# Three of eight residual tiles multiplied by the norm's factor on GpSimd

## The reference, cut to what matters

```python
def _rmsnorm(x, g):
    xf = x.astype(jnp.float32)
    y = xf * lax.rsqrt(jnp.mean(xf * xf, axis=-1, keepdims=True) + EPS)
    return (y * g.astype(jnp.float32)).astype(x.dtype)
...
            h = _rmsnorm(x, norm_pre_mix[i]) * (1.0 + sc1) + sh1
            mix, na, nb, ns = _token_mixer(h, ...)
            x = x + g1 * _rmsnorm(mix, norm_post_mix[i])
            h = _rmsnorm(x, norm_pre_ffn[i]) * (1.0 + sc2) + sh2
            ...
            x = x + g2 * _rmsnorm(f, norm_post_ffn[i])
```

## Time and profile before

| | |
|---|---|
| median of 3 executions | 2082.62 us (2078.98 to 2089.65) |
| profiled execution | 2081.15 us |
| its span in the profile | 2079.2 us |
| TensorE, VectorE, ScalarE, GpSimd busy | 93%, 59%, 41%, 10% of the span |
| first residual, Exp's end to the next norm's Ln | 505.83 to 519.83 us |
| second residual, the same | 941.63 to 955.63 us |
| third residual, the same | 1423.69 to 1437.69 us |

### The profile page before, as it was taken

One profiled execution on the slowest core, in us unless ns is written; L12 is line 12 of the kernel. 1 busy time (PEld: TensorE's weight loads), 2 busy tenths in 40 slices (PEclk: granted clock), 3 DMA queues, 4 the chain that ended last, 5 costly groups with the idle time before them and its releaser, 6 DMA issues.

```text
span 2079.2 us, 36179 instructions
## 1 busy us (share of the span) xinstructions
PE 1923.7 (93%) x13204; PEld 1709.5 (82%) x13204; DVE 1236.0 (59%) x1783; ACT 846.4 (41%) x1030; POOL 217.6 (10%) x317
## 2 busy tenths in 40 slices
PE   4999999989999999996999999896499999999994
PEld 3888989987899999995889989895387877888883
DVE  3677667645523223336776676555566566888886
ACT  4332222443422122225332222535355456777774
POOL 3101221200000000001102112100100000000020
PEclk9999999999999999998999999998699999999998
DMA  9642333353333233325724333323448566999994
GB/s 335 232 163 93 131 131 121 117 192 136 111 131 137 106 122 131 121 81 190 253 94 139 125 110 119 134 97 121 174 123 282 186 219 234 361 379 383 381 384 171
DMA packets 146667, 376.94 MB, mean 181 GB/s; under 512 B 9712, under 2 KB 47024, under 8 KB 146080
## 3 DMA queue, kind: packets, MB, share of 16 engines
q1 hardware_dynamic: 119824, 274.61, 38.4%
q0 software_dynamic: 26768, 101.28, 13.5%
HBM read 340.06 MB, written 35.80 MB: 181 GB/s over the span
## 4 chain that ended last, share of the span: by engine, by line
PE 81%; DVE 6%; DMA 5%; issue 4%; ACT 3%; POOL 1%; DVEq 0%; POOLq 0%; ACTq 0%; SPq 0%
PE ps L1913 35%; PE ps L1921 17%; PE ps L2216 15%; PE ps L2237 4%; DMA rawr<-w_gu 2%; PE ps L1934 2%; PE ps L2079 1%; DMA adaw<-w_ada 1%; PE ps L2067 1%; PE ps L2082 1%; PE ps L2080 1%; PE ps L1944 1%; DVE wlr L1746 1%; DVE wreg L1273 1%; PE ps L1953 1%
## 5 line engine op out<-in xcount | busy, mean ns | idle before, releaser
L1913 PE MATMUL ps<-h_hi,whi 128*128 128x272 f32 x2368 | 501.0, 293 | 17.3 <-DVE h_lo L1235 17.3
L1913 PE MATMUL ps<-h_lo,whi 128*128 128x272 f32 x2368 | 494.1, 290 | 0.0
L1913 PEld LDWEIGHTS ps<-h_hi,whi 128*128 128x128 f32 x2368 | 374.6, 190 | 62.4 <-issue 41.6
L1746 DVE TENSOR_TENSOR wlr<-rawr,whr 128x2048 fp32r<-128x2048 f32 (+1 forms) x162 | 321.9, 1992 | 121.6 <-ACT whr L1040 117.7
L1183 DVE TENSOR_TENSOR wlo<-raw,whi 128x1024 fp32r<-128x1024 f32 (+1 forms) x180 | 229.5, 1275 | 266.2 <-ACT whi L780 263.8
L1913 PEld LDWEIGHTS ps<-h_lo,whi 128*128 128x128 f32 x2368 | 375.0, 190 | 0.0
L780 ACT CAST whi<-raw 128x1024 fp32r<-128x1024 f32 (+1 forms) x180 | 193.6, 1076 | 356.6 <-PE ps L1921 356.6
L1040 ACT CAST whr<-rawr 128x2048 fp32r<-128x2048 f32 (+1 forms) x162 | 269.2, 1668 | 155.7 <-PE ps L2237 86.5
L1921 PE MATMUL ps<-h_hi,wlo 128*128 128x272 f32 x2368 | 320.5, 288 | 0.0
L1921 PEld LDWEIGHTS ps<-h_hi,wlo 128*128 128x128 f32 x2368 | 306.4, 188 | 0.0
L2216 PE MATMUL ps<-whr,hu_hi 128*128 128x512 f32 (+1 forms) x432 | 167.3, 387 | 7.2 <-DVE yu L1810 4.5
(11 more groups left out here) (405 smaller groups left out, 2604.7 us busy)
## 6 DMA issues: line engine op xcount, KB each, us to landing
rawr<-w_gu SPq DMA_DIRECT2D x90, 1024.0 KB, 9.4
adaw<-w_ada POOLq DMA_DIRECT2D x48, 1024.0 KB, 8.7
rawr<-w_dn SPq DMA_DIRECT2D x54, 768.0 KB, 9.9
raw<-w_mix SPq DMA_DIRECT2D x64, 512.0 KB, 3.6
raw<-w_gu SPq DMA_DIRECT2D x44, 512.0 KB, 3.4
raw<-w_out SPq DMA_DIRECT2D x32, 512.0 KB, 3.5
y_rows<-tables POOLq DMA_DIRECT2D x26, 512.0 KB, 2.9
raw<-w_xbc SPq DMA_DIRECT2D x24, 512.0 KB, 4.3
```

The costliest lines, as they stand in the source:

```text
L1746: v.tensor_tensor(ring_group(wlr, g).rearrange("p k s c -> p s k c"), raw_group(g), ring_group(whr, g).bitcast(F32).rearrange("p k s c -> ...
L1913: mm(ps[:, 2 * s + half, 0:HALF], whi[:, s, k * P:(k + 1) * P], a[:, k, half * HALF:(half + 1) * HALF], start=(n < 2), stop=False)
```

## The change

In the three residuals the products of tiles 5, 6 and 7 leave VectorE. GpSimd has a new function `late_tiles`, which waits for the same `rstd_ready` and makes these three products into the same places of `sq`, each with an increment of a new semaphore `late_scaled`. VectorE makes the first five products as before and waits for `late_scaled` ahead of the additions of tiles 5, 6 and 7. GpSimd's calls stand at the head of layer 1, ahead of the wait for x's spill (for the second residual), and in each layer after the wait for the windows (`windows_out`): in layer 0 that is behind the eight loads of modulation weights and ahead of the memset of the zeros.

```diff
         ADDED = {}
+        LATE, LATE_SET = (KT - 3, KT - 2, KT - 1), {(0, POST_MIX): 0, (0, POST_FFN): 1, (1, POST_MIX): 2}
...
         @block.gpsimd
         def _(pool):
+            def late_tiles(L, idx, src):
+
+                pool.wait_ge(rstd_ready, NORMS * L + idx + 1)
+                for k in LATE:
+                    nc.gpsimd.tensor_tensor(sq[:, k, 0:SEQ], src[:, k, 0:SEQ], rstd[:, 0:SEQ], ALU.mult
+                                            ).then_inc(late_scaled, 1)
+
...
             for L in range(DEPTH):
                 if L:
 
+                    late_tiles(0, POST_FFN, f)
                     pool.wait_ge(x_ready, 2 * KT * L)
                     pool.dma_start(x_spill, xreg[:, :]).then_inc(spill_out, 16)
...
                     pool.wait_ge(slabs_used, FIRST[0]["outB"] * 2 + PRIME)
                     ada_load(GAP, range(KT))
                 pool.wait_ge(windows_out, 64 * (L + 1))
+                late_tiles(L, POST_MIX, x)
                 if L == 0:
                     nc.gpsimd.memset(zeros, 0.0).then_inc(zero_made, 1)
...
                 for k in range(KT + 1):
 
-                    if k < KT:
+                    if k < KT and k not in LATE:
                         st.step(v.tensor_tensor(scaled[:, k, 0:SEQ], src[:, k, 0:SEQ], rstd[:, 0:SEQ], ALU.mult))
                         made.append(st.base + st.n)
                     if k:
-                        dve.wait_ge(dve_steps, made[k - 1])
+                        if k - 1 in LATE:
+                            dve.wait_ge(late_scaled, LATE_SET[L, idx] * len(LATE) + LATE.index(k - 1) + 1)
+                        else:
+                            dve.wait_ge(dve_steps, made[k - 1])
                         v.scalar_tensor_tensor(x[:, k - 1, 0:SEQ], scaled[:, k - 1, 0:SEQ], coef[:, k - 1, 0:1],
                                                old[:, k - 1, 0:SEQ], ALU.mult, ALU.add).then_inc(x_ready, 1)
```

More of the change, by code:

```diff
@@ L395, in hybrid_decoder @@
         smp_ready, t_ready, hhi_ready, h_ready = sem("smp_ready"), sem("t_ready"), sem("hhi_ready"), sem("h_ready")
-        x_ready = sem("x_ready")
+        x_ready, late_scaled = sem("x_ready"), sem("late_scaled")
         act_steps, dve_steps = sem("act_steps"), sem("dve_steps")
```

## The result

After: 2090.76 us, median of 20 runs (2085.31 to 2098.44). Before, timed beside it: 2081.60 us, median of 20 (2078.11 to 2090.18). The ratio is 1.0038 with a 95% interval of 1.0028 to 1.0048: the change costs 7.9 us (5.8 to 10.0). The forecast was 2089 us, in a range of 2080 to 2095, and a change within 0.5%; the measured median lies 1.8 us above it. The profiled execution of after has a span of 2088.9 us against 2079.2.

What follows compares the result with a forecast made beforehand. In the three residuals VectorE's products and additions were taken as the bound, with TensorE's sums nearly as late. Residual terms 1.0 + 2.8 + 2.8 = +6.6 us on the median of 2082.62 gave 2089 us, range 2080 to 2095.

Steps and rivals of the forecast that it cites:

- The hold: In each residual, GpSimd's three SBUF-reading products work in turn with VectorE and hold it 3.15 us, against 1.8 saved.
- All of it ahead of the first gated addition: Second and third residual: the whole 3.15 us falls before VectorE's first gated addition, about 6 us after Exp instead of 2.7.
- Second and third residual, +2.8 each: TensorE's first tile is late by 3.15 us, less 0.3 of idle, then its sums run without a gap: +2.8 each.
- the half clock has to be worked through from its first tile all the same: Second and third residual: TensorE's late start gives nothing back, as its first tiles run at half clock anyway.
- First residual, +1.0: GpSimd's set comes behind the weight loads; VectorE's last addition ends 1.5 us later, TensorE gives 0.5 back: +1.0.
- The removal alone: Three products fewer on VectorE per residual, without harm elsewhere: 1.0, 0.3 and 0.7 us gained, 2.0 in all, not 5.5.
- Waits and queues at nothing: VectorE's nine added waits in the second and third residual, and GpSimd's work queued behind its sets, cost nothing.
- No disturbance: Rival: GpSimd and VectorE don't disturb each other in these shapes; -2.0 us, 2080.6; chance 0.14.
- The set at the end: Rival: VectorE keeps GpSimd out until after the fifth tile, so the set falls last; +3.7 us, 2086.3; chance 0.10.
- The first product slow: Rival: each set's first GpSimd product is slow after DMA issues and holds VectorE; +12.0 us, 2094.6; chance 0.10.
- The sum: The three residuals together: 1.0 + 2.8 + 2.8 = +6.6 us, 2089.2 on the median; chance 0.62.

Runs made afterwards that it cites:

- e1: Kernel before, all products still on VectorE, plus three unread GpSimd products of constants in each residual; residuals 18.50, 17.03 and 17.01 us against 14.00 each.
- e8: The changed kernel unchanged, profiled once more for the spread; residuals 18.46, 16.95 and 17.27 us, sum +10.68.
- e10: The changed kernel unchanged, profiled a third time; residuals 15.57, 16.80 and 16.63 us, sum +7.00.
- e11: The changed kernel unchanged, profiled a fourth time; residuals 15.57, 16.83 and 16.36 us, sum +6.76.
- e7: Changed kernel without GpSimd's three products, plus 18 constant matmuls ahead of the second and third residual's sums; residuals 12.96, 12.97 and 12.96 us.
- e3: Changed kernel without GpSimd's three products, the semaphore only raised, so nobody makes them; residuals 13.70, 14.59 and 13.57 us, whole time not comparable.
- e2: Kernel before plus eight unread GpSimd memsets, which only write, beside VectorE in each residual; residuals 14.01, 14.02 and 14.00 us.
- e4: Changed kernel with GpSimd's set released by the first gated addition instead of the factor; residuals 15.57, 16.12 and 16.05 us.
- e6: Kernel before plus 13 constant matmuls ahead of the sums of the second and third residual; residuals 14.01, 14.00 and 14.01 us.
- e9: Changed kernel with the first residual's products given back to VectorE; 2089.42 us against 2082.59, ratio 1.0026; residuals 14.01, 17.73 and 16.74 us.
- e5: Changed kernel plus 18 constant matmuls ahead of the sums of the second and third residual; residuals 15.56, 16.58 and 16.53 us.

## Why the prediction was right, step by step

**The hold (3 x 1.05 = 3.15 us a set).** Right. 2.90 in the second residual, 3.13 in the first, 2.85 and 3.18 in e1. The product alone takes 1.24 us (e8), where 1.2 was taken and 1.0 to 1.3 were the bounds; e8's three are recorded with 1.26 to 1.28, and what lies above that in after, up to 1.73, is taken as GpSimd's own waits for VectorE. The Trainium skill, "SBUF — State Buffer", section "SBUF: two separate sides", would put the hold at the whole instruction, by estimate 3 x 1.24 = 3.7 a set. Where the two took turns the rows show less, 0.94 to 1.10 a product; in e8 they show 3.93 for the set.

**All of it ahead of the first gated addition.** Right: 5.59 us after Exp, where 2.68 + 3.15 = 5.83 follows from the terms ("about 6").

**Second and third residual, +2.8 each.** e10 and e11 give +2.80 and +2.83 in the second, the sum forecast, though two of its terms are off against one another: the first sum is late by 2.82 and 2.90 instead of 3.15, and the 32 sums take 9.66 and 9.61 instead of 9.68 less 0.3. In the profiled execution it was 2.90 and 10.17, +3.39. The step that was off is "the half clock has to be worked through from its first tile all the same", which took the half clock's length as fixed. It is not: here TensorE stayed at it from 951.41 to about 956.6, 5.2 us, where before had 3.75:

```profile
955.00:956.00 1.00, 1.00 (x3) 0.76 (x3) 1.00 (x3) 0.99 (x3) 0.00 (x0) 0.50 0.00 0
956.00:957.00 1.00, 1.00 (x4) 0.74 (x3) 1.00 (x2) 1.00 (x2) 0.00 (x0) 0.68 0.00 0
957.00:958.00 1.00, 1.00 (x6) 0.81 (x6) 0.44 (x3) 0.79 (x2) 0.70 (x2) 1.00 0.00 0
```

so its 32 sums took 10.17 instead of 9.68, with no idle left in them. In e11 the clock is up again 4.1 us after the first sum, with the same late start:

```profile
953.94 9.61 PE L1957 MATMUL ps<-wreg,cst 128*128 128x272 f32 x32 [9.90 <-ACT wreg L870]
...
957.00:958.00 1.00, 1.00 (x4) 0.77 (x3) 1.00 (x2) 0.98 (x2) 0.00 (x0) 0.50 0.00 0
958.00:959.00 1.00, 1.00 (x5) 0.83 (x5) 1.00 (x3) 0.99 (x2) 0.00 (x0) 0.98 0.00 0
```

With half of the time at half clock taken off, the sums of after and e11 come to the same 7.6 us (10.17 - 5.2 / 2 and 9.61 - 4.1 / 2). So in this residual the spread between executions of the same kernel is the clock's.

The third residual came out at +3.10, +3.27, +2.63 and +2.36, about the 2.8.

**First residual, +1.0.** +1.58 in three executions: the last addition was 1.3 later (1.5 forecast), but TensorE gave nothing of the 0.5 back. It ended 2.54 us behind the last addition against 2.27 in before, where the sums end at 511.14 + 8.65 = 519.79:

```profile
511.14 8.65 PE L1944 MATMUL ps<-wreg,cst 128*128 128x272 f32 x32
```

The spaced tiles in the middle left it idle (0.93, 0.49, 0.49), and the last three then came 0.67 apart and cost it 1.0 each. The fourth execution's +4.46 was in no rival: there the engines did not work in turn.

**The removal alone, -1.0, -0.3 and -0.7.** Mis-sized in the second and third. With full clock in the sums it is -1.03 in each (e7); with the clock as it falls, -0.30, +0.59 and -0.43 (e3). The sum of -2.0 lies between the two sums, -3.11 and -0.14, and the point of it held: nowhere did the 1.8 us of VectorE arrive. In after itself hardly any of it did: e1, with the same hold and all products still on VectorE, has +3.03 and +3.01 in the second and third residual, within the +2.36 to +3.39 of after's four executions.

**Waits and queues at nothing.** Right for the second and third residual: TensorE has no idle between its sums. GpSimd's next work there, x's spill, starts at 957.30 after a wait of 8.55 us for VectorE.

**The rivals.** No disturbance: excluded by e1 against e2. The set at the end: excluded, in the second and third residual the stretched operations are the samples' and the first product. The first product slow: the longest of the nine took 1.73, not 3. What the list lacked is the stall of e8, one rival with two steps, a set held at once and TensorE's clock lost to the wait, worth 2.9 us more in the first residual.

**The sum.** 6.6 forecast; the residuals gave 8.07, 10.68, 7.00 and 6.76 in four executions, 8.1 in the mean, and the timed runs 7.9 (5.8 to 10.0). The first residual (+1.58 for +1.0, and once +4.46) and the clock in the second and third took it above the forecast.

**What stays open.** Of the 9.7 us of span in the profiled execution 1.6 lie outside the residuals. The units of the mixer in layer 1 take 30.27 us or some 31 to 32, in other numbers from execution to execution: e2, whose residuals are those of before, took 470.8 us from the second residual's Ln to the third's Exp, before 468.06, after 471.28, e4 478.6, and e3 and e7, in which GpSimd makes no products, 472.23 and 471.66. So the products are not needed for the longer units; whether the change makes them likelier was not settled. Why e8's addition stood still is open as well.

**No better version.** The best that this idea could give is e7's residuals, 3.1 us or 0.15%, with products that cost nothing and with extra matmuls. e6, before with those matmuls, has unchanged residuals. Nothing was found that beats before.

## What to carry to other kernels

Before a product is moved from VectorE to GpSimd, look whether both engines read SBUF with it: here each product that GpSimd took saved VectorE 0.61 us and held it for about 1.0, and 1.8 us of less work on an engine that wasn't alone on the path was worth 1.0 at best. Where a chain starts (first tile, then sums without a gap), a hold ahead of its first link is paid in full; work that must be moved was a little cheaper behind that link (e4, 0.3 to 1.3 us of 3 in one execution). Work that only writes, like the memsets of e2, can stand beside VectorE's two-input operations at no cost.

## What the runs showed of the hardware that was not expected

An operation of VectorE that is already running can stand still through three GpSimd instructions in a row: 0.74 us became 4.67 in e8, though by the recorded starts the addition had begun 0.41 before the first of them. The Trainium skill, "SBUF — State Buffer", section "SBUF: two separate sides", says that whichever of the two starts first has the shared pair of ports for its whole instruction. In e8 the one that began first was the one that stood still, so the trace differs.

TensorE's time at half clock (1.2 GHz) after 7 to 10 us of idle was not the same from one execution to the next, in the same residual: 3.75 us in before, 5.4 in e3, 5.2 in after, 4.1 in e11, 6.0 in e9. In e1, e5 and e8 it had been full when TensorE took up its sums again, behind idles of 2.16, 2.16 and 4.00 us, and fell to half while the sums ran; in e5 that was 0.7 us after the first of them.
